# Sixteen sums of squares on the tensor engine: one full-precision product each, or two in the rounded format over a high and a low part

## The reference, cut to what matters

```python
def rmsnorm(x, w):
    xf = x.astype(jnp.float32)
    y = xf * lax.rsqrt(jnp.mean(xf * xf, axis=-1, keepdims=True) + EPS) * w.astype(jnp.float32)
    return y.astype(x.dtype)

# in gated_deltanet_branch, q = l2norm(q) * A_HEAD_DIM ** -0.5
o = chunk_gated_delta_rule(q, k, v, g, beta)
o = rmsnorm(o, o_norm) * jax.nn.silu(z.reshape(Bsz, T, A_HEADS, A_HEAD_DIM).astype(jnp.float32))
```

## Time and profile before

| | |
|---|---|
| median of three runs | 1315.19 us (1314.4 to 1316.35) |
| the profiled execution's own time | 1316.84 us |
| its span, first to last instruction | 1314.9 us |
| PE busy | 1273.2 us, 97% |
| DVE, ACT, POOL busy | 949.3, 688.1, 587.3 us |
| mean granted TensorE clock | 0.994 of full |

### The profile page before, as it was taken

The page is one execution under the profiler, slowest core; times in us unless marked ns, Lnnn a source line. Parts: engine busy times, 40 slices in busy tenths (PEclk is TensorE's granted clock), DMA queues, the critical chain, the costliest instruction groups (busy, mean ns, idle before and its releaser), DMA issues.

```text
span 1314.9 us, 18307 instructions
## 1 busy us (share of the span) xinstructions
PE 1273.2 (97%) x6797; PEld 1061.9 (81%) x6797; DVE 949.3 (72%) x1685; ACT 688.1 (52%) x1112; POOL 587.3 (45%) x380
## 2 busy tenths in 40 slices
PE   7998999999999999999998999999999999998997
PEld 5787888888888888888876788888888888886786
DVE  5588788888788888884349767787878777787413
ACT  6345355464546364644336566666666666755203
POOL 6534253443334333422127694646556474622400
PEclk9999999999999999999999999999999999999999
DMA  7310111201111110234215011311111111218503
GB/s 185 90 41 24 33 49 33 64 17 49 49 49 49 49 49 17 71 118 150 80 52 187 2 32 33 93 52 49 49 49 49 49 49 49 80 51 286 176 0 128
DMA packets 106856, 91.40 MB, mean 70 GB/s; under 512 B 3105, under 2 KB 92306, under 8 KB 106770
## 3 DMA queue, kind: packets, MB, share of 16 engines
q1 hardware_dynamic: 106770, 90.25, 22.6%
HBM read 66.65 MB, written 23.59 MB: 69 GB/s over the span
## 4 chain that ended last, share of the span: by engine, by line
PE 82%; DVE 7%; ACT 6%; issue 2%; POOL 2%; DMA 1%; SPq 0%; DVEq 0%; ACTq 0%
PE psum L530 28%; PE psum L685 19%; PE psum L699 5%; PE psum L2561 5%; PE psum L2535 3%; PE psum L2548 2%; PE psum L2443 2%; PE psum L547 2%; PE psum L658 2%; DVE stick L2122 1%; PE psum L2464 1%; PE psum L2391 1%; PE psum L2426 1%; PE psum L2474 1%; ACT late L1341 1%
## 5 line engine op out<-in xcount | busy, mean ns | idle before, releaser
L530 PE MATMUL psum<-u_hi,w_hi 128*128 128x512 f32 x640 | 260.8, 407 | 4.0 <-POOL w_lo L497 1.6
L530 PE MATMUL psum<-u_hi,w_lo 128*128 128x512 f32 x640 | 258.4, 404 | 0.0
L530 PE MATMUL psum<-u_lo,w_hi 128*128 128x512 f32 x640 | 258.1, 403 | 0.0
L497 POOL TENSOR_TENSOR w_lo<-w_raw,w_hi 128x1024 fp32r<-128x1024 f32 (+1 forms) x45 | 105.9, 2354 | 258.5 <-ACT w_hi L492 246.2
L530 PEld LDWEIGHTS psum<-u_hi,w_hi 128*128 128x128 f32 x640 | 121.2, 189 | 29.4 <-issue 4.1
L530 PEld LDWEIGHTS psum<-u_hi,w_lo 128*128 128x128 f32 x640 | 121.1, 189 | 23.8 <-issue 1.7
L530 PEld LDWEIGHTS psum<-u_lo,w_hi 128*128 128x128 f32 x640 | 121.2, 189 | 20.8 <-issue 0.5
L1816 DVE SCALAR_TENSOR_TENSOR late<-raw,cols,late 128x1024 f32<-128x1024 f32 x72 | 119.2, 1655 | 1.9
L627 POOL TENSOR_TENSOR w_lo<-w_raw_b,w_hi 128x512 fp32r<-128x512 f32 x40 | 58.4, 1460 | 113.2 <-ACT w_hi L611 113.2
L2122 DVE TENSOR_TENSOR_SCAN stick<-soft 128x1024 f32<-128x1024 f32 (+3 forms) x64 | 104.2, 1628 | 0.2
L492 ACT ACTIVATE w_hi<-w_raw 128x1024 fp32r<-128x1024 f32 (+1 forms) x45 | 46.0, 1022 | 101.7 <-PE psum L530 101.5
(11 more groups left out here) (309 smaller groups left out, 3216.1 us busy)
## 6 DMA issues: line engine op xcount, KB each, us to landing
w_raw<-in_a_w_in SPq DMA_DIRECT2D x33, 512.0 KB, 4.1
w_raw<-in_b_w_in SPq DMA_DIRECT2D x16, 512.0 KB, 5.5
w_raw_b<-in_b_w_in SPq DMA_DIRECT2D x16, 512.0 KB, 5.4
b_rows<-o_part SPq DMA_DIRECT2D x14, 512.0 KB, 3.9
o_rows<-o_part_a SPq DMA_DIRECT2D x12, 512.0 KB, 3.6
x_stage<-in_x SPq DMA_DIRECT2D x8, 512.0 KB, 7.4
out<-fin_o SPq DMA_DIRECT2D x8, 512.0 KB, 2.6
u_lo<-b_rows SPq DMA_DIRECT2D x7, 512.0 KB, 8.4
```

Of the source, the lines that this page charges most:

```text
L497: G.tensor_tensor(lo_tiles(key), raw_tiles(key), hi_tiles(key).bitcast(F32), ALU.subtract).then_inc(lo_done, 1)
L530: mm = PE.matmul(psum[:, half], (w_hi, w_hi, w_lo)[part][:, buffer(key), k], (u_hi, u_lo, u_hi)[part][:, k, half * HALF:(half + 1) * HALF] ...
```

## The change

Each of the sixteen sums of `o_sq` becomes two products in the rounded format. ScalarE copies `o_sq` to `o_sq_hi` (`upper_o`), VectorE subtracts (`lower_o`) into `o_sq_lo`, and TensorE multiplies each part with `ones_r`. Both parts lie in the tile `sq_hi`, which the keys' squares have left by then. One semaphore, `o_split`, counts the three steps of a half in order (added, high, low); those who waited for the addition wait for its first step. The new instructions have fixed places: for half 0, `upper_o` in slot 13 of ScalarE behind `v_new` and ahead of `square_q` and `inv_first`, and `lower_o` in slot 12 of VectorE behind `invT` and ahead of `tokens` (for the last head, behind `add_q`); for half 1, `upper_o` in slot 0 of ScalarE behind the logarithm, and `lower_o` in slot 0 of VectorE behind taps 8 and 9.

```diff
+        o_sq_hi, o_sq_lo = sq_hi[:, 0:HALF], sq_hi[:, HALF:T]
...
-        o_added = sig("o_added", 2)
+        o_split = sig("o_split", 6)
+        O_ADDED, O_HI, O_LO = 1, 2, 3
...
+            def upper_o(t, half):
+                o_split.wait(act, t, 3 * half + O_ADDED)
+                A.activation(o_sq_hi, o_sq[:, :], ACT.Copy).then_inc(o_split.handle, 1)
...
                     A.activation(v_new[:, :], psum[:, 2, P:2 * P], ACT.Copy).then_inc(vn_done.handle, 1)
                 if s == 12:
                     square_o(t, 0)
+                if s == 13:
+                    upper_o(t, 0)
...
                     if t + 1 < H:
                         prepare(t + 1, s)
+                    if s == 0 and t >= 1:
+                        upper_o(t - 1, 1)
...
+            upper_o(H - 1, 1)
             norm_scale(H - 1, 1)
...
+            def lower_o(t, half):
+                o_split.wait(dve, t, 3 * half + O_HI)
+                V.tensor_tensor(o_sq_lo, o_sq[:, :], o_sq_hi.bitcast(F32), ALU.subtract).then_inc(o_split.handle, 1)
...
+                    if h > 0:
+                        lower_o(h - 1, 0)
                     tokens(h, 0)
...
+                    if s == 12 and t == H - 1:
+                        lower_o(t, 0)
                     if s == 0 and t >= 1:
                         add_q(t - 1, 1)
...
+                    if s == 0 and t >= 1:
+                        lower_o(t - 1, 1)
...
             for i in range(2):
                 add_output(i, LAST_GROUP + i, 16 * (KB - HOME))
+                if i == 0:
+                    lower_o(H - 1, 1)
...
             def sum_squares_o(t, half):
-                o_added.wait(pe, t, half + 1)
-                PE.matmul(psum[:, SUM_BANK], ones[:, :], o_sq[:, :], start=True, stop=True).then_inc(osum_ready.handle, 1)
+                o_split.wait(pe, t, 3 * half + O_LO)
+                for i, part in enumerate((o_sq_hi, o_sq_lo)):
+                    mm = PE.matmul(psum[:, SUM_BANK], ones_r[:, :], part, start=i == 0, stop=i == 1)
+                mm.then_inc(osum_ready.handle, 1)
```

More of the change, by code:

```diff
@@ L1331, in square_q @@
                     if h > 0:
-                        o_added.wait(act, h - 1, 1)
+                        o_split.wait(act, h - 1, O_ADDED)
                 elif h > 1:
-                    o_added.wait(act, h - 2, 2)
+                    o_split.wait(act, h - 2, 3 + O_ADDED)
                 silu_kq.wait(act, h, 2)
@@ L1874, in add_q @@
                 V.tensor_tensor(o_sq[:, :], o_sq[:, :], q_sq_first[:, :] if half == 0 else q_sq_second[:, t % 2], ALU.add
-                                ).then_inc(o_added.handle, 1)
+                                ).then_inc(o_split.handle, 1)
+            def lower_o(t, half):
+                o_split.wait(dve, t, 3 * half + O_HI)
+                V.tensor_tensor(o_sq_lo, o_sq[:, :], o_sq_hi.bitcast(F32), ALU.subtract).then_inc(o_split.handle, 1)
             def norm_o(t, half):
```

## The result

The changed kernel takes **1329.65 us** (median of four runs, 1329.48 to 1330.74) where the kernel before takes 1315.65 us beside it (1314.4 to 1316.35). The ratio is 1.011, with a 95% interval of 1.0098 to 1.0122: it is slower by 1.1%. The forecast was 1327.1 us, in a range of 1320 to 1333. Profiled execution against profiled execution it is 1329.77 to 1316.84, +12.9 us, where the sum of the prediction said +11.9.

A forecast was written before the change was run, and what follows sets the result against it. TensorE's order of work was taken to set the time. Terms 8.6 - 0.4 (half 1, head 6) + 0.9 + 0.7 + 1.1 + 1.0 = +11.9 us on the median 1315.19 gave 1327.1 us, range 1320 to 1333.

The forecast's parts named there:

- Half 1 of heads 0 to 5: Six sums: VectorE's subtraction behind taps 8 and 9 makes TensorE wait 1.58 us; +1.44 us each, +8.6 us.
- Half 0: Heads 0 to 6: ScalarE's copy delays inv_first by 0.52 us, less 0.395 gained; +0.125 us each, +0.9 us.
- The wait in slot 16: VectorE's update of the inverse late for ScalarE's packing: 0 to 0.35 us each, 0.1 taken, +0.7 us.
- Head 6's half 0: GpSimd's subtraction of weights at 591.21 holds VectorE's added subtraction, making it and k_tail late; +1.1 us, nothing at low end.
- Half 0 of head 7: Copy and subtraction come between add_q and the sum TensorE already waits for; +1.0 us.
- The last sum: Subtraction behind VectorE's addition ends about 681.76; the sum ends at 682.52 where 682.53 stood; 0.
- The gain did not stay: Rival: waits are made up later and all sixteen sums give 0.395 us; -6.3 us, 1308.9 us; chance 0.05.
- the delays spread: Rival: one further handover a head late by 0.68 us, 4.8 us on top; +16.7, 1331.9 us; chance 0.13.
- Tap 8 did not escape: Rival, half 1 of heads 0 to 5: tap 8 no longer held by GpSimd; +0.9, 1316.1 us; chance 0.13.
- in part: Rival: tap 8 escapes in some of six heads, 1.84 us less each; with three, 1321.6 us; chance 0.03.

The follow-up runs named there:

- e3: Changed kernel with half 1's subtraction on VectorE ahead of tap 8 instead of behind taps 8 and 9; 1318.18 us, ratio 1.0027.
- e6: Changed kernel, VectorE's order kept, with GpSimd's subtraction of weights begun only after half 1's low part; 1319.43 us, ratio 1.0026.
- e4: Changed kernel with ScalarE's copy of half 0 in slot 12, behind the squaring, instead of slot 13; 1324.91 us, ratio 1.0072.
- e10: Changed kernel with VectorE's low part for the stored inverse's half 1 moved from slot 13 to slot 11; 1327.76 us, ratio 1.009.
- e2: Changed kernel with the split made and waited for, but each sum one full-precision product as before; 1334.29 us, ratio 1.0146.
- e11: Changed kernel with GpSimd's last-head slot 23 weight subtraction waiting for the last low part, and the stored inverse's half 1 low part in slot 11; 1325.47 us.
- e1: Changed kernel without the split: two rounded products read unfilled tiles and TensorE waits only for the addition; 1309.79 us, ratio 0.9955.

## Why the prediction was right

**Half 1 of heads 0 to 5, +8.6 us: right, mechanism and size.** The low part was forecast for 205.03 to 205.71 and ran from 204.95 to 205.63; TensorE's start for 205.75, and it was 205.78; +1.44 us each, and it was +1.50. The 0.26 us that a product costs more after a wait were there: 0.70 us, against 0.46 to 0.49 in the chain where it doesn't wait. e3 and e6 each took the wait away and with it 10 to 11.5 us.

**Half 0, +0.9 us: right.** The chain piece of the turn moved by the length of the copy, and e4 took it back. TensorE's wait ahead of the turn, forecast at 0.8 us, was 3.9 / 7 = 0.56 us.

**The wait in slot 16, +0.7 us: the mechanism right, the term mis-sized.** It measured 1.6 us, outside none of the forecast's bounds (0 to 0.35 us each). The step gave VectorE a margin of 0.1 us at ScalarE, and there was none: the packing started 0.44 us after the update before, and 0.45 us after it now. It also took most of VectorE's delay as made up by then; 0.40 us more than TensorE's own was left. So ScalarE came 0.41 us late against TensorE, and the turn took 0.32 us longer, in five of the seven heads. e4 and e10 show that it comes from VectorE's work of slots 12 and 13; e2 shows that it takes back 1.7 us of the products' gain.

**Head 6's half 0, +1.1 us: wrong.** No hold of VectorE came. The times were right: the step had VectorE's subtraction at 591.20 and GpSimd's at 591.21, and they started in that order, 0.01 us apart. But the step let VectorE pay, as in rows 11, where GpSimd had started first. Here it was GpSimd's that got longer, 2.37 us instead of 1.82, and nothing waited for it:

```profile
602.50 0.69 DVE L1891 TENSOR_TENSOR sq_hi<-o_sq,sq_hi 128x512 fp32r<-128x512 f32 x1
...
602.51 2.37 POOL L500 TENSOR_TENSOR w_lo<-w_raw,w_hi 128x768 fp32r<-128x768 f32 x1 [12.37 <-DVE invT L2006]
```

**Half 0 of head 7, +1.0 us: right.** TensorE stood 2.11 us where it had stood 0.72, and the sum took 0.73 instead of 1.12.

**The last sum, 0: wrong.** It measured +1.4 us. The step looked at VectorE's queue and not at GpSimd's, which already in the kernel before had a subtraction of weights running over the forecast place, 681.04 to 681.76 (timeline of GpSimd, kernel before):

```profile
680.19 2.40 POOL L497 TENSOR_TENSOR w_lo<-w_raw,w_hi 128x1024 fp32r<-128x1024 f32 x1 [7.22 <-ACT w_hi L492]
```

The prediction named the rule (a subtraction with two SBUF inputs can be held as well) and applied it in head 6, where it didn't happen, and not here, where it did. The two errors, -1.1 and +1.4, nearly cancel. That is luck: each alone would have moved the sum by over a microsecond, beside the 0.9 us that slot 16 lacked. e11 shows the length of 0.69 us with GpSimd out of the way.

**The rivals.** The gain did not stay: e1 gives it (1309.79), and the changed kernel is 19.9 us above that. The wait in slot 16 is a small case of "the delays spread": one handover per head late by 0.32, not by 0.68 us. Tap 8 did not escape in any of the six heads, neither in all nor in part; that it costs the large term is what e6 shows.

## What to carry to other kernels

On an engine that sets the time, the price of a shorter instruction is where its new inputs are made. Two products gave 6 us, and two elementwise instructions behind the wrong neighbours cost 20; the same instructions, one ahead of a held tap and one a slot earlier, with the last head left as it was, gave 3.8 us. Look in the trace at both VectorE and GpSimd beside every place where an instruction is added, and leave the old form where the engine already stands waiting for that very input.

## What the runs showed of the hardware that had not been expected

In the pairs of instructions read here the one that starts second is held, with starts down to 0.01 us apart. VectorE's TENSOR_SCALAR takes 2.95 us when GpSimd began 0.01 us ahead, and 0.75 us when it didn't. The TENSOR_TENSOR of two SBUF inputs takes 2.09 us with GpSimd already running (last sum), 1.48 us when GpSimd has 0.93 us left to run (e3), and 0.69 us when it is first; then GpSimd's takes 2.37 instead of 1.82 us (head 6). The held instruction of VectorE ends 0.55 to 0.56 us after GpSimd's in all three cases (203.72 to 203.16, 695.07 to 694.51, 201.86 to 201.31). In e6 GpSimd's starts 0.17 us behind tap 10, and takes 3.38 instead of 2.40. The page GPSIMD Engine Reference of the Trainium skill ("Specifications") has the two engines contend when VectorE's instruction is in a two-port mode or has two SBUF inputs. The runs agree for the subtractions and for tap 10, which have two. Tap 8 has one input of this size and is held as well; no row shows in which mode it is.
